# Gate rows multiplied by g_post before they are spread, and a new written-out order for the end of the mLSTM layer

## The reference, cut to what matters

```
sh, sc, gt = silu(cvec) @ w_ada + b_ada            # for the latent and for the context tokens
h = rmsnorm(x, g_pre) * (1 + sc) + sh
y = mixer(h)                                       # ends in  (hh * silu(z)) @ w_out
x = x + gt * rmsnorm(y, g_post)
```

```
hh = hsum * sigmoid(o)                             # per token, 4 heads of 256
hh = rmsnorm(hh, g_head)                           # per head
y  = (hh * silu(z)) @ w_out
```

## Time and profile before

| | us |
|---|---|
| median of 3 runs | 1534.04 (1533.65 to 1538.38) |
| the profiled execution | 1533.56, its span 1531.7 |
| PE busy | 1449.0 (95%) |
| DVE busy | 992.6 (65%) |
| ACT busy | 759.3 (50%) |
| mean granted TensorE clock | 0.993 of full speed |

### The profile page before, as it was taken

The page is one execution under the profiler, slowest core; times in us unless marked ns, Lnnn a source line. Parts: engine busy times, 40 slices in busy tenths (PEclk is TensorE's granted clock), DMA queues, the critical chain, the costliest instruction groups (busy, mean ns, idle before and its releaser), DMA issues.

```text
span 1531.7 us, 24151 instructions
## 1 busy us (share of the span) xinstructions
PE 1449.0 (95%) x9368; PEld 1196.1 (78%) x9368; DVE 992.6 (65%) x2317; ACT 759.3 (50%) x1674; POOL 70.8 (5%) x82
## 2 busy tenths in 40 slices
PE   6999999999999999999988999998899899899999
PEld 4787766788778777888766787666787799699987
DVE  4657677564667548535585678767867477777753
ACT  4446566453655443342134546656657346455542
POOL 0000000010000000020000100001101020000000
PEclk9999999999999999999999999999999999999999
DMA  9132270322640322222361155243544633445554
GB/s 367 59 110 83 91 272 11 103 83 69 255 172 1 108 92 83 96 83 83 145 227 55 56 178 154 98 119 125 177 139 137 221 130 107 151 163 182 192 182 135
DMA packets 58882, 202.84 MB, mean 132 GB/s; under 512 B 6818, under 2 KB 9930, under 8 KB 58640
## 3 DMA queue, kind: packets, MB, share of 16 engines
q1 hardware_dynamic: 52928, 192.84, 36.0%
q10 hardware_dynamic: 5440, 7.07, 2.0%
q0 software_dynamic: 400, 1.38, 0.3%
HBM read 199.43 MB, written 1.84 MB: 131 GB/s over the span
## 4 chain that ended last, share of the span: by engine, by line
PE 70%; DVE 16%; ACT 5%; issue 3%; DMA 3%; POOL 2%; SPq 0%; ACTq 0%; DVEq 0%; POOLq 0%
PE ps L2282 65%; PE ps L2285 5%; DVE w_l L2945 3%; DVE st L3052 2%; ACT w_h L2599 1%; DMA w_l_ada<-in_l_ada 1%; DVE l_P L2949 1%; ACT l_P L2602 1%; DVE l_h_lat L2953 1%; DVE x L2953 1%; DMA w_raw<-in_l_out 1%; DVE m_P L3536 1%; DVE l_xn L2949 1%; DMA w_raw<-in_m_merge 1%; POOL mstat L3630 1%
## 5 line engine op out<-in xcount | busy, mean ns | idle before, releaser
L2945 DVE TENSOR_TENSOR w_l<-w_raw,w_h 128x1024 fp32r<-128x1024 f32 (+3 forms) x263 | 315.6, 1206 | 78.1 <-ACT w_h L2599 77.5
L2599 ACT ACTIVATE w_h<-w_raw 128x1024 fp32r<-128x1024 f32 (+3 forms) x263 | 272.2, 1042 | 100.0 <-DMA w_raw<-in_f_down 25.3
L2282 PE MATMUL ps<-w_h,l_hTh 128*128 128x512 f32 (+1 forms) x384 | 155.4, 405 | 1.2 <-issue 0.6
L2282 PE MATMUL ps<-w_l,l_hTh 128*128 128x512 f32 (+1 forms) x384 | 150.8, 393 | 0.0
L2282 PE MATMUL ps<-w_h,l_hTl 128*128 128x512 f32 (+1 forms) x384 | 150.8, 393 | 0.0
L2602 ACT ACTIVATE l_P<-ps,st 128x512 f32<-128x512 f32 (+1 forms) x128 | 77.6, 608 | 87.7 <-DVE st L2953 60.1
L2282 PE MATMUL ps<-f_hTh,w_h 128*128 128x256 f32 x352 | 99.5, 283 | 0.0
L2282 PE MATMUL ps<-f_hTh,w_l 128*128 128x256 f32 x352 | 98.9, 281 | 0.0
L2282 PE MATMUL ps<-f_hTl,w_h 128*128 128x256 f32 x352 | 98.9, 281 | 0.0
L2282 PE MATMUL ps<-l_hTh,w_h 128*128 128x512 f32 (+1 forms) x264 | 96.9, 367 | 0.6 <-issue 0.6
L2282 PE MATMUL ps<-l_hTl,w_h 128*128 128x512 f32 (+1 forms) x264 | 96.5, 366 | 0.0
(11 more groups left out here) (448 smaller groups left out, 3443.6 us busy)
## 6 DMA issues: line engine op xcount, KB each, us to landing
w_two<-in_l_ada SPq DMA_DIRECT2D x24, 1024.0 KB, 6.5
w_raw<-in_l_z SPq DMA_DIRECT2D x32, 512.0 KB, 3.6
w_two<-in_l_adg SPq DMA_DIRECT2D x16, 1024.0 KB, 5.0
w_raw<-in_l_out SPq DMA_DIRECT2D x32, 512.0 KB, 3.6
w_raw<-in_m_merge SPq DMA_DIRECT2D x24, 512.0 KB, 3.3
w_raw<-in_f_gate SPq DMA_DIRECT2D x22, 512.0 KB, 3.2
w_raw<-in_f_up SPq DMA_DIRECT2D x22, 512.0 KB, 3.2
w_raw<-in_f_down SPq DMA_DIRECT2D x22, 512.0 KB, 4.3
```

Of the source, the lines that this page charges most:

```text
L2282: return p.e.matmul(out, lhsT, rhs, start=start, stop=stop)
L2599: return p.e.activation(out, a, func, scale=scale)
L2945: return p.e.tensor_tensor(out, a, b, op)
```

## The change

- `g_post` is loaded as 32 partitions x 256 columns for each of the four blocks of `gt_rows` (four small DMAs, now from POOL's queue), DVE multiplies `gt_rows` (128x256) by it before `gate_split`, and `gate_spread` becomes a plain copy of the bank: on ACT for all four in layer 2, in the other layers two on ACT and two on DVE.
- In `ada` the gate's steps come at ticks 5, 7, 8, 9, 10 instead of 5 to 9, and the banks of the spreads and of the turned modulation can come from a pool of their own (`spare`).
- `finish` is cut into `rows_of` (up to `fin_rows`) and `turned` (the transposes and on). The order at the end of `layer_mlstm` is written out: context rows within steps 4 and 5, context columns kp 0 and 1 within steps 6 and 7, the latent gates and squares, the roundings and the spreads at fixed places after that, with `spare` and `turns` widened by banks 3, 4, 6, 7 and 5 once the steps are over.
- In `turn` the first half of `l2_out` takes the two context tiles together (block by block), and the latent turns are put in after three of its four blocks.

```
-    def ada(p, pool, groups, gate=None, lag=2, blocks=(), late=None):
+    def ada(p, pool, groups, gate=None, lag=2, blocks=(), late=None, steps=(5, 7, 8, 9, 10), spare=None):
-                wait += [[5 + x, lambda x=x: gate.step(x, pool)] for x in range(5)]
+                wait += [[steps[x], lambda x=x: gate.step(x, spare)] for x in range(5)]
...
     def turn(p, i, og, post, rows, order=(LAT, CTX), beside=None):
-        half = p.dense_tok(f"l{i}_out", 0, 8, 2, 512, og, singles(first + second), post.evac(0))
+        groups = [first] + singles(second) if beside else singles(first + second)
+        half = p.dense_tok(f"l{i}_out", 0, 8, 2, 512, og, groups, post.evac(0))
         if beside:
-            weave(beside, upto(half, 8), 8, 14)
+            drain(upto(half, 6))
+            for _ in range(2):
+                drain(upto(beside, 2))
+                drain(upto(half, 1))
+            drain(beside)
...
-        gate, ctx = Gate(p, 2, *gate, f), m.finish(CTX, f, (2,))
-        mod = p.ada(PAIR, [(3, 0), (2, "gate"), (3, 1)], gate)
-        drain(braid(upto(steps, 6), upto(mod, 6), upto(ctx, 3)))
+        spare, turns = [*PAIR], [2]
+        gate, ctx = Gate(p, 2, *gate, f), chain(m.rows_of(CTX), m.turned(CTX, f, turns))
+        mod = p.ada(PAIR, [(3, 0), (2, "gate"), (3, 1)], gate, steps=(3, 5, 6, 8, 9), spare=spare)
+        drain(braid(upto(steps, 6), upto(ctx, 5), upto(mod, 6)))
         gate.free = p.fence()
-        drain(braid(steps, mod, ctx))
-        p.W.split_to(len(p.W.order) + 1, len(p.W.order) + 1)
+
+        def tail():
+            yield from upto(steps, 2)
+            next(steps)
+            m.gate_lat(1)
+            yield
+            next(steps)
+            p.fin_sq(m, 1)
+            yield
+        drain(braid(upto(tail(), 4), upto(ctx, 4), upto(mod, 4)))
+        drain(steps)
+        spare += [3, 4, 6, 7]
+        turns += [5]
+        p.rows_rstd4(m, 1)
+        m.gate_lat(0)
+        next(ctx), next(mod), next(ctx)
+        w = len(p.W.order) + 1
+        p.W.split_to(w, w - 1)
+        next(mod)
+        p.W.split_to(w + 1, w)
+        next(ctx), next(ctx)
+        next(mod)
+        p.W.split_to(w + 1, w + 1)
+        next(mod)
+        p.W.split_to(w + 2, w + 1)
+        p.fin_sq(m, 0)
+        p.W.split_to(w + 2, w + 2)
+        p.rows_rstd4(m, 0)
+        p.fin_rows(m, 1)
+        next(mod), drain(mod)
+        p.W.split_to(w + 3, w + 3)
+        p.fin_rows(m, 0)
+        drain(ctx)
         f = p.fence()
-        lat = m.finish(LAT, f, TRANS)
+        lat = m.turned(LAT, f, TRANS)
...
+    def gate_lat(self, t):
+        self.p.fin_o(self, t, [self.htok[t, h] for h in range(4)])
...
 (ACT)
     def gate_split(p, gate, gt_tok):
-        p.wait_ge(gt_tok, gate.free)
+        p.wait_ge(("gate", "g", gate.i), gate.free)
         p.copy(gate.gth[:], p.n.gt[:]).then_inc(*p.mark("gate", "h", gate.i))
+    def gate_spread(p, gate, bank, lc, b, tok, key):
+        if gate.i == 2 or b == 0:
+            p.wait_ge(tok, gate.free)
+            p.copy(gate.G[lc][:, b * 512:b * 512 + 512], p.n.bank(bank)).then_inc(*p.mark(*key))
 (DVE)
     def gate_split(p, gate, gt_tok):
+        p.wait_ge(gt_tok, ("d_gpost", gate.i))
+        p.tt(p.n.gt[:], p.n.gt[:], gate.gpost[:], ALU.mult).then_inc(*p.mark("gate", "g", gate.i))
         p.wait_ge(("gate", "h", gate.i))
...
     def gate_spread(p, gate, bank, lc, b, tok, key):
-        p.tt(gate.G[lc][:, c], p.n.bank(bank), gate.gpost[:, c], ALU.mult).then_inc(*p.mark(*key))
+        if gate.i != 2 and b:
+            p.wait_ge(tok, gate.free)
+            p.copy(gate.G[lc][:, b * 512:b * 512 + 512], p.n.bank(bank)).then_inc(*p.mark(*key))
 (POOL; the one on ACT goes)
+    def gate_load(p, gate, free):
+        p.wait_ge(free)
+        for j in range(4):
+            src = p.n.dram[f"l{gate.i}_g_post"][256 * j:256 * j + 256].unsqueeze(0).to_broadcast([32, 256])
+            p.e.dma_start(gate.gpost[32 * j:32 * j + 32, :], src).then_inc(*p.landed("d_gpost", gate.i, of=4))
```

More of the change, by code:

```diff
@@ L541, in dense_ch @@
                 yield True
-    def ada(p, pool, groups, gate=None, lag=2, blocks=(), late=None):
-        wait, blocks = [], list(blocks)
+    def ada(p, pool, groups, gate=None, lag=2, blocks=(), late=None, steps=(5, 7, 8, 9, 10), spare=None):
+        wait, blocks, spare = [], list(blocks), spare or pool
         def tick():
@@ L574, in ada @@
                 p.ada_row(v, bank, s, w, key, p.stage_tok[s])
-                then = lambda i=i, g=g, s=s, v=v, w=w: p.ada_mod(i, g, s, w, v, pool)
+                then = lambda i=i, g=g, s=s, v=v, w=w: p.ada_mod(i, g, s, w, v, spare)
                 if late is None:
@@ L755, in ends @@
         G = [at(f"G{x}", [128, D], F32, k) for x, k in enumerate((g0, g1))]
-        gpost, gth = at("gpost", [128, D], F32, gpost), at("gth", [128, 256], F32R, gth)
+        gpost, gth = at("gpost", [128, 256], F32, gpost), at("gth", [128, 256], F32R, gth)
         junk, yg = [at(f"junk{x}", [128, 512], F32, junk + 2 * x) for x in range(2)], at("yg", [128, ntiles, D], F32, yg)
@@ L1774, in chunks, with rows_of @@
             yield
-    def finish(self, pair, fence, pool):
+    def gate_lat(self, t):
+        self.p.fin_o(self, t, [self.htok[t, h] for h in range(4)])
+    def rows_of(self, pair):
         p = self.p
-        hf_tok = [None, None]
         for t in pair:
@@ L1788, in finish, with turned @@
             p.fin_rows(self, t)
-            yield
+        yield
+    def turned(self, pair, fence, pool):
+        p = self.p
+        hf_tok = [None, None]
         for kp in range(4):
@@ L2906, in ff_high @@
         p.copy(m.ff.h[:, k, :], m.ft[k % 4][:]).then_inc(*p.mark("ffn", "high", k))
[L2908 to L2911, removed]
     def ml_tables(p, m, fence):
@@ L2998, in gate_spread @@
     def gate_spread(p, gate, bank, lc, b, tok, key):
-        c = slice(b * 512, b * 512 + 512)
-        p.wait_ge(tok, ("d_gpost", gate.i), gate.free)
-        p.tt(gate.G[lc][:, c], p.n.bank(bank), gate.gpost[:, c], ALU.mult).then_inc(*p.mark(*key))
+        if gate.i != 2 and b:
+            p.wait_ge(tok, gate.free)
+            p.copy(gate.G[lc][:, b * 512:b * 512 + 512], p.n.bank(bank)).then_inc(*p.mark(*key))
     def rows_mean(p, rows, t):
```

## The result

| | before | after |
|---|---|---|
| median of the runs of one comparison, us | 1535.70 (1533.65 to 1538.71, 6 runs) | 1526.16 (1523.65 to 1531.48, 6 runs) |
| the profiled execution, us | 1533.56 | 1528.67 |

The ratio is 0.9947, 95% interval 0.9933 to 0.9961: the kernel became 0.5% faster. The changed kernel was measured twice more, with 0.9935 (0.9916 to 0.9953) and 0.9936 (0.9923 to 0.9948). 1525.0 was forecast, with a range of 1520.5 to 1531.0.

What follows compares the result with a forecast made beforehand. PE was taken as the bound, held up at the mLSTM's end by late DVE; -8.4 there and -0.9 in layer 3 took the profiled 1533.56 to 1524.3, put at 1525 for the runs, range 1520.5 to 1531.

Steps and rivals of the forecast that it cites:

- The DVE list: End of the mLSTM: DVE's work in its new order, weight block 0 ready at about 799.7 and latent rows at about 808.0.
- 813.7: End of the mLSTM: forecast start of latent tile 0 of `l2_out`, against 822.14 before, a gain of 8.4 us.
- No half clock: Sign of being right: no half clock on PE between step 5 and the first latent tile.
- rival (b): Gap before weight block 0: clock falls, the dense pair begins at 1.2 GHz, some 3 us of gain lost, 1528; chance 0.10.
- the 3.9 us: End of the mLSTM on DVE: latent rows stand at about 808.0 instead of 811.93.
- the 2.93 before block 2: PE's stop before weight block 2, claimed gone since blocks 1 and 2 are ready at 802 and 804.
- one stop of 2.06: PE's wait for an eviction of G at the mLSTM's end, claimed to be ended by more banks for the spreads.
- second account of the 3.9: DVE cross-check: 5.6 from context rows and G products, 0.8 from POOL's wait, less 0.35, 0.7 and 1.2.
- rival (a): End of the mLSTM: moved context work delays the recurrence in full, latent rows at 812, gain 4.4, time 1529.5; chance 0.14.
- rival (c): Layer 1: four g_post transfers come one after another, DVE stands, up to 6.7 us lost, 1531; chance 0.05.
- The -0.9 of layer 3: Layer 3's gate: spreads change engine, DVE is tighter there, PE's 1.30 wait for the high part covered; gain 0.9 us.
- (d): End of the mLSTM: ACT becomes late with the rounding of block 3, slower, 1536 at 12 late; chance 0.05.

## Why the prediction was right

**The DVE list.** Step by step it came out as worked out. `h` of step 6 was put at 782.1 and started at 781.93; block 0 was to be ready at 799.7, and its rest ends at 799.4; `fin_rows` of tile 0 was to end at 808.0, and ends at 807.5. The wait before step 7 was put at 1.2 and is 0.65 + 0.43. These hits hide two differences that cancelled: the execution started step 4 1.4 sooner than the kernel before, and 1.4 was lost at 756.39 to POOL, which no step of mine had.

**PE.** The pair starts at 799.54 (799.8 forecast), and latent tile 0 at 814.03 (813.7). The idle time is 4.8 instead of the 3 that I named: 2.60 before the pair, where I had 1 to 2, and 1.54 at 760.51, the held DVE instruction. That 813.7 was hit within 0.4 is partly luck. From the pair to latent tile 0 I had 13.9, with four turns at 0.6 each; at full clock the stretch takes 12.95, since 48 matmuls are 11.2 of it and the turns add only 1.75. The half clock that I had ruled out added 1.53 in the profiled execution. Counted from step 4's start, the forecast was 813.7 - 754.04 = 59.66; the profiles show 61.37, 59.84 and 61.36, a gain of 6.7, 8.3 and 6.7 where I had 8.4.

**The clock.** "No half clock" failed in two profiles of three. In 800 to 804 the clock is 0.57 of full speed in the changed kernel. My ground against rival (b), that a stop of 2.06 alone had left the clock at 1.00 in the kernel before, was one observation of something that falls out differently from run to run.

**Which part brings the gain.** The total was right, the account behind it was not. I wrote that four products of G gone from DVE were part of the 3.9 us by which the latent rows come sooner. They are, on DVE (1.5), but as built the first latent tile gains nothing by it: M with the gate of before is 59.65, and the load's place in POOL's queue takes back what the gate frees. I gave the 2.93 before block 2 to the pairs and the roundings together; the runs give the pairs 0.74 and the roundings 1.28. I named banks for one stop of 2.06; taken away from the new order, they cost 5.57. The four parts that were undone one at a time come to 1.43 + 5.57 + 1.28 + 0.74 = 9.0, against 8.26 for M from before to the change at full clock; they need not add up, since two lists race, and the early context rows and the early gates of the latent tiles were never undone alone. Two side sums of the prediction do not close either: the second account of the 3.9 comes to 4.15, and the 1529.5 of rival (a) leaves out the 0.9 of layer 3.

**The load on POOL.** I priced its landing (2 us of cover in layer 1: no wait was seen, and rival (c) with its 6.7 did not happen) and forgot what stands behind it in POOL's queue in layer 2. That is the step of the prediction that failed, though the total held: the load was moved to POOL's queue, and I looked at the load and not at the queue. Its price is 1.40 us at DVE, and 1.45 in M.

**The other layers.** The -0.9 of layer 3 was not found. PE's stop of 1.30 for the high part is gone from the stretch that answers to the earlier trace rows (the largest stops there are 0.86 and 0.83, as before), yet from latent tile 0 to the last output of layer 3 it is 214.17 and 212.83 us in two profiles of the change, against 212.46 before. PE's idle time in this stretch is in fact less (13.48 and 12.26, against 14.01), but its busy time is longer (200.69 and 200.57, against 198.45). The two profiles of the change have a half-clock spell there that the kernel before has not, behind a stop of 1.69 for ACT that stands in the kernel before as well (1.70, at a clock of 1.00). In the first profile:

```profile
929.48 0.54 PE L2330 MATMUL ps<-identr,l_qs 128*128 128x128 f32 x4 [1.69 <-ACT l_PTs L2644]
929.48:933.00 3.52, 3.52 (x16) 2.52 (x18) 3.02 (x8) 2.54 (x6) 0.00 (x0) 0.59 0.34 128
```

Over all profiles, from latent tile 0 to the first dense matmul of the next network, the twelve with the new gate take 211.2 to 214.2 and the two with the old one 212.6 and 212.4. A gain of 0.9 would not stand out among them.

**Rivals (a) and (d).** Neither showed: the latent rows came at 807.5 and not at 812, and ACT sat idle for 6.15 us after its last rounding before the latent turns, so it was far from late.

**What stays open.** The three comparisons give 8 to 10 us by their ratios (9.5 to 10.6 by the medians), and 6.7 to 8.3 of them are in M. Where the rest comes from is not shown; it is within what changes between executions of the same code: in the first profile of the change the stretch from 1101.60 to 1292.40 took 190.80 us at a clock of 0.97, in the second 187.00 at 0.99, and nothing in it was edited. Which is why the profiled execution gained only 4.9 where M gained 6.7.

```profile
1101.60:1292.40 190.80, 179.64 (x1412) 160.91 (x1413) 122.89 (x362) 107.91 (x250) 19.63 (x15) 0.97 0.46 145
```

```profile
1098.70:1285.70 187.00, 176.61 (x1411) 158.01 (x1412) 122.84 (x362) 107.80 (x250) 19.64 (x15) 0.99 0.46 148
```

## What to carry to other kernels

When two engines race to one point, write both lists down with their durations, and undo each part of the change alone before crediting any: here the part that looked like housekeeping (five more banks) was worth more than the one that took work off the tight engine. Before the clock's share is taken off a time, look whether another engine's list would have filled it. When an instruction with a wait is moved to another engine's queue, read that queue from the new place on, since whatever stood behind is now behind the wait too. And compare a stretch that holds the change rather than whole executions, when the clock alone moves these by several microseconds.

## What the runs showed of the hardware

- A product on POOL (128x512, 1.05 us) held a DVE instruction of 128x4 with two SBUF inputs for 1.40 us, 1.56 in place of 0.16, in nine of nine profiles of kernels that issue the load ahead of that product, and in none of the five others.
- After a stop of 2.25 to 2.60 us before the same dense matmuls, TensorE's clock fell to 1.2 GHz for a part of them in four of seven profiles; of the changed kernel alone, in two of three. It cost 1.5 us over 12.95. In layer 3 it fell behind a stop of 1.69 in a profile of the changed kernel (0.59 over 3.52 us) and not behind one of 1.70 in that of the kernel before.
- Sixteen issues of a DMA from POOL took 0.50 us at the median and 0.69 at most in the profile of the changed kernel, with landings of 2.0 to 6.3 us. In layer 1 DVE was busy for 1.39 of the 2.02 us of four such issues.
